# The PEER gate map of a streaming-encoder layer: from one-hot matmuls on TensorE to indirect writes of per-expert totals

## The chip, the cores and the metric

The kernel runs on one core of one Trainium2 chip. The time is that of one execution on the device, in microseconds. A program on one core has one span; the time of an execution is a little longer than that span, since starting and ending it is counted too.

## What is computed

The layer takes 512 frames of 1024 numbers (and 16 meta tokens), runs a token mixer, and then the part that this change touches, a product-key layer of 16384 single-neuron experts ("PEER"). Everything is float32. Cut to what matters:

```python
def peer(x, w_q, sub_keys, u_emb, v_emb):        # x: (512, 1024)
    # two times top 16 of 128 keys for each of 8 heads, then top 16 of their 256 sums
    eidx = ...                                   # (512, 8*16) expert numbers i1*128 + i2
    gate = softmax(sc)                           # (512, 8*16)
    a = einsum('nd,ned->ne', x, u_emb[eidx])     # u: (16384, 1024)
    coef = gelu(a) * gate
    return einsum('ne,ned->nd', coef, v_emb[eidx])
```

One frame can pick the same expert in two heads; then both gates count.

## The kernel before

The kernel doesn't gather for the first 384 frames (`DENSE`, three blocks of 128). It computes all 16384 experts for them: an **up pass** of 128 tiles (a tile is 128 experts), each a product of 24 matmuls of 128x512 (8 slices of the 1024 numbers, three float32r passes each, `three_pass`, L342), a gelu (L1185) and a store to DRAM; then a **down pass** of 128 experts' tiles with 18 matmuls each (L344 to L346 again, from `v_hi`, `v_lo`, `c_hi`, `c_lo`), which adds coefficient times `peer_v` into six PSUM banks. The coefficient is gelu times gate, where the gate is a **gate map** in DRAM: for each (i2, i1) of the 128 x 128 experts a row of 384 frames, nearly all zeros. The last 128 frames go another way: their rows of `peer_v` are gathered by 128 indirect DMAs (L1919) and their activations by 128 more (L1925), all issued by GpSimd during the down pass, and VectorE adds them up (L1703).

Before the up pass stands `route` (L1194), in which queries, key scores and the two top-16 stages run, with the first 24 up tiles between them. Its tail works block by block: VectorE compares (`hits`), GpSimd multiplies (L1517), VectorE sums (`sums`, L1435) into `picked`, the numbers i1 and i2 of every slot. TensorE then transposes i1, i2 and gates of the block (L1317 to L1319) and ScalarE copies them to `i1_t`, `i2_t`, `g_t`. Three up tiles stand between two such blocks.

In `experts` (L1565) VectorE splits the gates into three bfloat16 parts, and in each of the first 24 steps it builds one-hot rows for 16 frames (L1654, L1657, L1660); TensorE turns them into 16 frames of gate map with 48 matmuls of 128x128 in bfloat16 (L1754); ScalarE copies four banks to `gate_stage` (L1798); SyncE stores them (L1858). The last 32 up tiles never go to DRAM: VectorE multiplies them at once by their gates (`keep`, L1669) and keeps them in SBUF as `resident_coef`. The down pass takes those 32 first (`order`), so it can begin with no load but `peer_v`, and its first four tiles are split during the last eight up tiles.

Order on each engine is the order of the code. An engine's instructions wait on semaphores; SyncE issues nearly all loads and stores in one queue, so what stands behind a wait of its waits too. Two raw slots, two hi and two lo slots carry the up tiles; `RING` = 4 slots carry `v_raw`, `v_hi`, `v_lo`, `act_in` and `gate_in` in the down pass.

## Time and profile before

| | us |
|---|---|
| median of 3 runs | 1928.85 |
| lowest and highest | 1923.22, 1933.78 |
| the profiled execution's own time | 1916.39 |
| its span | 1914.5 |
| TensorE matmuls busy | 1815.5 (95%) |
| VectorE busy | 1184.6 (62%) |
| ScalarE busy | 668.0 (35%) |
| GpSimd busy | 579.2 (30%) |

The stages, by the trace: mixer and projections to about 464 us, `route` to 742, one-hot steps to 949, the rest of the up pass to 1379, the down pass to 1902, and a last norm. The granted clock of TensorE was 0.971 of full in the mean. The profile's page gives busy time by engine and by 40 slices of the span; a group is all instructions of one line, operation and tile. Busy time of TensorE is not work at its peak, since matmuls overlap: a matmul of 0.39 us starts every 0.227 us.

### The profile page before, as it was taken

To read this page: it belongs to the slowest core of one execution; us is meant where nothing else is said; L and a number is where in the kernel's file an instruction comes from. 1 tells how busy PE (TensorE), PEld (TensorE's weight loads), DVE (VectorE), ACT (ScalarE), POOL (GpSimd) and SP (SyncE) were. 2 spreads that over 40 slices of the span, in tenths; PEclk is the share of its full clock that TensorE was granted. 3 is DMA by queue.
4 is the path that set the end of the run, shared out by engine and by line. 5 is a ranking of instruction groups with operands and counts; after the bars stand their busy time and mean duration, and the time that the engine had idled before them with its cause. 6 is when DMAs were issued, how large, how long until landed. Compare 5 with 4: busy or idle time off the path is not lost. (4 is left out here: it accounts for less than half of the span.)

```text
span 1914.5 us, 24469 instructions
## 1 busy us (share of the span) xinstructions
PE 1815.5 (95%) x8991; PEld 1491.0 (78%) x8991; DVE 1184.6 (62%) x2275; ACT 668.0 (35%) x1004; POOL 579.2 (30%) x422
## 2 busy tenths in 40 slices
PE   5999999988999689999999999999999999999997
PEld 4877867866788467888888888888888888888885
DVE  3259945542799977888622222232467888888885
ACT  4333203342332223666532222222343333333332
POOL 3644300010544550000000000000177777777820
PEclk9999996988999889999999999999999999999998
DMA  4322110051232333789884444455488999999992
GB/s 136 100 66 56 45 31 1 1 176 55 83 105 78 89 100 109 177 210 235 209 222 148 148 140 146 151 148 188 138 294 269 362 364 372 376 362 372 366 340 88
DMA packets 241690, 337.63 MB, mean 176 GB/s; under 512 B 119856, under 2 KB 178608, under 8 KB 241472
## 3 DMA queue, kind: packets, MB, share of 16 engines
q1 hardware_dynamic: 219088, 269.60, 45.6%
q0 software_dynamic: 22528, 67.19, 9.7%
q8 instruction: 29, 0.48, 0.1%
q14 instruction: 45, 0.37, 0.1%
HBM read 282.19 MB, written 54.53 MB: 176 GB/s over the span
## 5 line engine op out<-in xcount | busy, mean ns | idle before, releaser
L344 PE MATMUL psum<-x_hi,ts_hi_u 128*128 128x512 f32 x1024 | 405.9, 396 | 22.1 <-DVE ts_lo_u L1157 18.9
L346 PE MATMUL psum<-x_hi,ts_lo_u 128*128 128x512 f32 x1024 | 402.4, 393 | 0.0
L345 PE MATMUL psum<-x_lo,ts_hi_u 128*128 128x512 f32 x1024 | 402.2, 393 | 0.0
L1919 POOL DMA_INDIRECT sparse_rows<-in_peer_v,sparse_v_row x128 | 161.5, 1262 | 752.1 <-PE psum L346 662.2
L1157 DVE TENSOR_TENSOR ts_lo_u<-ts_raw_u,ts_hi_u 128x1024 fp32r<-128x1024 f32 x117 | 157.9, 1350 | 370.5 <-ACT ts_hi_u L1152 370.1
L345 PE MATMUL psum<-v_lo,c_hi 128*128 128x512 f32 x768 | 298.8, 389 | 0.0
L346 PE MATMUL psum<-v_hi,c_lo 128*128 128x512 f32 x768 | 298.8, 389 | 0.0
L344 PE MATMUL psum<-v_hi,c_hi 128*128 128x512 f32 x768 | 298.8, 389 | 0.0
L1819 ACT ACTIVATE v_hi<-v_raw 128x1024 fp32r<-128x1024 f32 x128 | 135.8, 1061 | 316.0 <-PE psum L346 276.1
L1185 ACT ACTIVATE ut_out_u<-psum 128x512 f32<-128x512 f32 x128 | 76.6, 598 | 484.1 <-PE psum L346 373.9
L344 PEld LDWEIGHTS psum<-x_hi,ts_hi_u 128*128 128x128 f32 x1024 | 194.6, 190 | 63.5 <-DVE ts_lo_u L1157 19.3
L346 PEld LDWEIGHTS psum<-x_hi,ts_lo_u 128*128 128x128 f32 x1024 | 194.3, 190 | 41.4
L345 PEld LDWEIGHTS psum<-x_lo,ts_hi_u 128*128 128x128 f32 x1024 | 194.5, 190 | 40.0
L1685 DVE TENSOR_TENSOR v_lo<-v_raw,v_hi 128x1024 fp32r<-128x1024 f32 x128 | 157.0, 1226 | 94.3 <-ACT v_hi L1819 71.7
L1925 POOL DMA_INDIRECT sparse_act<-up_acts_sparse,sparse_act_at x128 | 176.1, 1376 | 39.0 <-issue 39.0
L344 PEld LDWEIGHTS psum<-v_hi,c_hi 128*128 128x128 f32 x768 | 144.1, 188 | 30.1
L346 PEld LDWEIGHTS psum<-v_hi,c_lo 128*128 128x128 f32 x768 | 144.1, 188 | 29.9
L345 PEld LDWEIGHTS psum<-v_lo,c_hi 128*128 128x128 f32 x768 | 144.1, 188 | 29.9
L1152 ACT ACTIVATE ts_hi_u<-ts_raw_u 128x1024 fp32r<-128x1024 f32 x128 | 135.1, 1056 | 15.2 <-DMA ts_raw_u<-in_peer_u 15.1
L1157 POOL TENSOR_TENSOR ts_lo_wq<-ts_raw_wq,ts_hi_wq 128x1024 fp32r<-128x1024 f32 x16 | 38.5, 2408 | 291.0 <-ACT ts_hi_wq L1152 290.9
L344 PE MATMUL psum<-whi_in,h_hi 128*128 128x512 f32 (+1 forms) x280 | 110.2, 394 | 2.2 <-PEq L244 2.2
L345 PE MATMUL psum<-wlo_in,h_hi 128*128 128x512 f32 (+1 forms) x280 | 107.9, 385 | 0.0
(231 smaller groups left out, 2636.3 us busy)
## 6 DMA issues: line engine op xcount, KB each, us to landing
ts_raw_u<-in_peer_u SPq DMA_DIRECT2D x128, 512.0 KB, 3.8
v_raw<-in_peer_v SPq DMA_DIRECT2D x128, 512.0 KB
gate_map<-gate_stage SPq DMA_DIRECT2D x48, 512.0 KB, 5.7
up_acts<-ut_out_u SPq DMA_DIRECT2D x96, 192.0 KB, 1.9
act_in<-up_acts SPq DMA_DIRECT2D x96, 192.0 KB
gate_in<-gate_map SPq DMA_DIRECT2D x96, 192.0 KB
raw_in<-in_w_in SPq DMA_DIRECT2D x56, 256.0 KB, 2.8
ts_raw_wq<-in_peer_wq SPq DMA_DIRECT2D x16, 512.0 KB, 4.1
```

Source lines behind the costliest of these rows:

```text
L344: nc.tensor.matmul(out, l_hi, r_hi, start=first, stop=False)
L345: nc.tensor.matmul(out, l_hi, r_lo, start=False, stop=False)
L346: return nc.tensor.matmul(out, l_lo, r_hi, start=False, stop=last)
L1152: nc.scalar.activation(self.hi[:, slot], self.raw[:, slot], ACT.Copy).then_inc(self.hi_done, 1)
L1157: eng_ops.tensor_tensor(self.lo[:, slot], self.raw[:, slot], self.hi[:, slot].bitcast(F32), ALU.subtract).then_inc(self.lo_done, 1)
L1185: nc.scalar.activation(self.out[:, slot], self.bank[slot], ACT.Gelu).then_inc(self.bank_read, 1)
L1685: nc.vector.tensor_tensor(dn.v_lo[:, i], dn.v_raw[:, i], dn.v_hi[:, i].bitcast(F32), ALU.subtract).then_inc(v_lo_done, 1)
L1819: nc.scalar.activation(dn.v_hi[:, i], dn.v_raw[:, i], ACT.Copy).then_inc(v_hi_done, 1)
L1919: nc.gpsimd.indirect_dma_start(dn.rows[:, r], None, v_rows, bass.IndirectOffsetOnAxis(sparse["v_row"][:, j:j + 1], 0)).then_inc(row_in[r], 16)
L1925: nc.gpsimd.indirect_dma_start(dn.picked[:, j:j + 1], None, places, bass.IndirectOffsetOnAxis(sparse["act_at"][:, j:j + 1], 0)).then_inc(p ...
```

## The change

The gate map is made without TensorE. In `route`, GpSimd clears a tile of zeros and SyncE writes it over the whole map in 32 stores of 768 KB, two behind each of the 16 routing steps. `route` keeps `picked` as expert numbers (`expert`) and as addresses in the map (`gate_at`); transposes and their copies go. In `experts`, VectorE makes for every slot of the first 384 frames one `scalar_tensor_tensor` over the 128 slots of its frame: 1 where the other slot has the same expert, times its gate, summed into `total`. So all slots that name one expert hold the same total, and GpSimd writes them with 384 indirect DMAs of 128 x 4 bytes, in whatever order they land. The map is the same as before.

`resident_coef` goes too: all 128 tiles are stored, the down pass goes in the order 0 to 127 and loads gelu and gate for each. `v_raw`, `act_in` and `gate_in` get 8 slots (`RAW`). The first four down tiles are split around the last up tile, and SyncE loads the first coefficients only when all 384 writes have landed.

```diff
@@ route, SyncE
+            sp.wait_ge(zeros_done, 1)
             for j in range(2, G + 2):
                 load_q(j)
...
                 for t in ups[n]:
                     next_up(t)
+                for x in range(n * ZERO_STORES // STEPS, (n + 1) * ZERO_STORES // STEPS):
+                    store_zeros(x)
@@ route, TensorE (and its three copies on ScalarE)
-                pe.wait_ge(picked_done, b + 1)
-                nc.tensor.transpose(bank[:, 0:P], picked[:, b % 2, 0].rearrange(flat), ident[:])
-                nc.tensor.transpose(bank[:, P:2 * P], picked[:, b % 2, 1].rearrange(flat), ident[:])
-                nc.tensor.transpose(bank[:, 2 * P:3 * P], gates[:, b].rearrange(flat), ident[:]).then_inc(turned, 1)
@@ experts, VectorE
+            def total_gate(m, b, j):
+                if m >= 2:
+                    dve.wait_ge(totalled, m - 1)
+                nc.vector.scalar_tensor_tensor(out=dn.same[:, j % 2], in0=expert[:, b], scalar=expert[:, b, j:j + 1],
+                                               in1=gates[:, b].rearrange("p h k -> p (h k)"), op0=ALU.is_equal,
+                                               op1=ALU.mult, accum_out=dn.total[:, b, j:j + 1]).then_inc(totalled, 1)
...
             for n in range(TILES):
-                if n < STEPS:
-                    one_hots(n, n % 2)
                 if n + 2 < TILES:
                     ut.split_lo(nc.vector, dve, n + (R + 2), n % 2)
-                if n >= FIRST_KEPT:
-                    keep(n)
-                if n >= LEAD and (n - LEAD) % 2:
-                    low((n - LEAD) // 2)
+                for m in range(n * TOTALS, min((n + 1) * TOTALS, DENSE_BLOCKS * SLOTS)):
+                    total_gate(m, *place(m))
+            for e in range(EARLY):
+                product(e)
+                low(e)
@@ experts, TensorE
-                    ut.product(nc, pe, x_hi, x_lo, it * 2 + (R + par + 1), 1 - par, False)
-                    rows(it * 2 + par, par, False)
+                    ut.product(nc, pe, x_hi, x_lo, it * 2 + (R + par), par, False)
@@ experts, ScalarE
+            for n in range(TILES):
+                if n == TILES - 1:
+                    for e in range(EARLY):
+                        split_down(e)
                 finish_up(n)
                 next_split(n)
@@ experts, SyncE
-                if n == LEAD - 2:
-                    for e in range(RING):
+                if n == TILES - 2:
+                    for e in range(RAW):
                         load_v(e)
+                    for b in range(DENSE_BLOCKS):
+                        sp.wait_ge(scattered[b], 16 * SLOTS)
+                    for i in range(2):
+                        sp.wait_ge(ut.stored[i], 16 * (RAW // 2))
+                    for e in range(RAW):
+                        load_coef(e)
                 ut.store(sp, acts_d, acts_s, R + n, n % 2)
@@ experts, GpSimd
+            pool.wait_ge(zeroed, 16 * ZERO_STORES)
+            for m in range(DENSE_BLOCKS * SLOTS):
+                b, j = place(m)
+                h, k = divmod(j, PEER_TOPK)
+                if h and k == 0:
+                    pool.wait_ge(scattered[b], 16 * PEER_TOPK * h)
+                pool.wait_ge(totalled, m + 1)
+                scatter_gate(b, j)
             pool.wait_ge(ut.product_done, NKEYS)
```

What this moves is shown at three places, as the instructions stand in a row on one engine. First VectorE at the start of `experts`, before (`val` and `one` are the one-hot tiles, `ts_lo_u` the low half of an up tile):

```order
L1638 TENSOR_TENSOR g_part_b<-g_rest,g_part_f 128x384
L1710 CAST key_twice<-i_t 128x384 x4
L1713 COPY g_twice<-g_part_b 128x384 x6
L1157 TENSOR_TENSOR ts_lo_u<-ts_raw_u,ts_hi_u 128x1024
L1654 TENSOR_TENSOR one<-iota_b,key_twice 128x2048
L1657 TENSOR_TENSOR one<-iota_b,key_twice 128x2048
L1660 TENSOR_TENSOR val<-one,g_twice 128x2048 x3
L1157 TENSOR_TENSOR ts_lo_u<-ts_raw_u,ts_hi_u 128x1024
```

And the same place now:

```order
L1152 TENSOR_TENSOR ts_lo_u<-ts_raw_u,ts_hi_u 128x1024 x2
L1591 SCALAR_TENSOR_TENSOR same_expert,gate_total<-expert,gates 128x128 x10
L1152 TENSOR_TENSOR ts_lo_u<-ts_raw_u,ts_hi_u 128x1024
L1591 SCALAR_TENSOR_TENSOR same_expert,gate_total<-expert,gates 128x128 x10
L1152 TENSOR_TENSOR ts_lo_u<-ts_raw_u,ts_hi_u 128x1024
```

The conversions and the one-hot tiles are gone, and behind each `ts_lo_u` stand ten short sums, until 384 are made. Second, SyncE's queue where up pass and down pass meet, before:

```order
L1869 DMA up_gate<-gate_map 128x384
L1875 DMA v_raw<-in_peer_v 128x1024 x4
L1191 DMA up_acts_sparse<-ut_out_u 128x128
L1145 DMA ts_raw_u<-in_peer_u 128x1024
L1869 DMA up_gate<-gate_map 128x384
```

That piece stands ten tiles ahead of the end of the up pass. The same queue now, two tiles ahead of its end:

```order
L1185 DMA up_acts_sparse<-ut_out_u 128x128
L1725 DMA v_raw<-in_peer_v 128x1024 x8
L1732 DMA act_in<-up_acts 128x384
L1733 DMA gate_in<-gate_map 128x384
L1732 DMA act_in<-up_acts 128x384
L1733 DMA gate_in<-gate_map 128x384
```

The first coefficients (`act_in`, `gate_in`) stand behind eight loads of 512 KB and behind the wait for GpSimd's writes. Third, GpSimd's own order from the end of `route` into `experts`, before (a branch is the passage from one block of the program to the next):

```order
L1517 TENSOR_TENSOR hit<-hit,idx_f 128x2048 x8
L1255 UNCONDITIONAL_BRANCH
L1909 UNCONDITIONAL_BRANCH
L1919 DMA sparse_rows<-in_peer_v,sparse_v_row 128x1024 x4
L1925 DMA sparse_act<-up_acts_sparse,sparse_act_at 128x1 x8
```

and now:

```order
L1509 TENSOR_TENSOR hit<-hit,idx_f 128x2048 x8
L1249 UNCONDITIONAL_BRANCH
L1756 UNCONDITIONAL_BRANCH
L1779 DMA gate_map<-gate_total,gate_at 6291456x1 x384
L1767 DMA sparse_rows<-in_peer_v,v_row 128x1024 x4
```

All 384 writes stand ahead of the first gathered row.

## Rows read from the trace of the kernel before

**Rows 1.** The page, by 40 slices: TensorE busy, in tenths.
```profile
PE   5999999988999689999999999999999999999997
```

**Rows 2.** Windows: busy us (x instructions) of each engine, clock, DMA share, GB/s.
```profile
800.00:850.00 50.00, 50.00 (x436) 42.90 (x435) 43.50 (x39) 33.17 (x38) 0.00 (x0) 1.00 0.94 229
1000.00:1050.00 50.00, 50.00 (x223) 41.39 (x222) 12.04 (x10) 13.92 (x19) 0.00 (x0) 1.00 0.47 146
1600.00:1650.00 50.00, 50.00 (x223) 41.39 (x222) 43.26 (x54) 19.01 (x26) 37.38 (x28) 1.00 1.01 371
```

**Rows 3.** ScalarE by time: gelus that end up tiles (start, us, engine, line).
```profile
764.40 0.60 ACT L1185 ACTIVATE ut_out_u<-psum 128x512 f32<-128x512 f32 x1 [2.83 <-PE psum L346]
772.64 0.60 ACT L1185 ACTIVATE ut_out_u<-psum 128x512 f32<-128x512 f32 x1 [2.81 <-PE psum L346]
...
1324.91 0.60 ACT L1185 ACTIVATE ut_out_u<-psum 128x512 f32<-128x512 f32 x1 [3.89 <-issue]
1330.35 0.60 ACT L1185 ACTIVATE ut_out_u<-psum 128x512 f32<-128x512 f32 x1 [3.89 <-issue]
```

**Rows 4.** Tail of `route`, TensorE: the first of three transposes, a slowed matmul, the next block.
```profile
678.64 0.33 PE L1317 MATMUL psum<-ident,picked 128*128 128x128 f32 x1 [2.43 <-DVE picked L1435]
...
679.69 0.63 PE L346 MATMUL psum<-x_hi,ts_lo_u 128*128 128x512 f32 x1
...
743.40 0.47 PE L344 MATMUL psum<-x_hi,ts_hi_u 128*128 128x512 f32 x1 [2.05 <-PEq L1255]
```

**Rows 5.** The same tail, ScalarE: gelus of its third and its last up tile, and the next.
```profile
676.25 0.60 ACT L1185 ACTIVATE ut_out_u<-psum 128x512 f32<-128x512 f32 x1 [24.70 <-PE psum L346]
...
741.39 0.60 ACT L1185 ACTIVATE ut_out_u<-psum 128x512 f32<-128x512 f32 x1 [3.89 <-PE psum L346]
...
750.72 0.60 ACT L1185 ACTIVATE ut_out_u<-psum 128x512 f32<-128x512 f32 x1 [7.79 <-PE psum L346]
```

**Rows 6.** VectorE: short operations over 128 slots, and the low half of an up tile.
```profile
739.22 0.28 DVE L1445 SCALAR_TENSOR_TENSOR act_row<-picked 128x128 f32<-128x128 f32 x1
739.42 0.28 DVE L1447 TENSOR_TENSOR frame_diag<-ident,iota 128x128 f32<-128x128 f32 x1
...
1326.49 1.23 DVE L1157 TENSOR_TENSOR ts_lo_u<-ts_raw_u,ts_hi_u 128x1024 fp32r<-128x1024 f32 x1 [3.75 <-ACT ts_hi_u L1152]
```

**Rows 7.** GpSimd's indirect DMAs: the whole group, then two single ones.
```profile
L1925 POOL DMA_INDIRECT sparse_act<-up_acts_sparse,sparse_act_at x128 | 176.1, 1376 | 39.0 <-issue 39.0
...
1385.29 0.95 POOL L1925 DMA_INDIRECT sparse_act<-up_acts_sparse,sparse_act_at  x1 [0.30 <-issue]
...
1403.69 1.57 POOL L1925 DMA_INDIRECT sparse_act<-up_acts_sparse,sparse_act_at  x1 [0.31 <-issue]
```

**Rows 8.** SyncE's queue and ScalarE in `route`: one load, and the split that needs it.
```profile
529.46 0.44 SPq L1145 DMA_DIRECT2D ts_raw_wq<-in_peer_wq  x1
...
534.88 1.05 ACT L1152 ACTIVATE ts_hi_wq<-ts_raw_wq 128x1024 fp32r<-128x1024 f32 x1
539.86 0.60 ACT L1185 ACTIVATE ut_out_u<-psum 128x512 f32<-128x512 f32 x1 [3.92 <-PE psum L346]
```

**Rows 9.** SyncE's loads of `v_raw` and the `ts_raw_u` behind, and its reader.
```profile
1328.58 1.86 SPq L1875 DMA_DIRECT2D v_raw<-in_peer_v  x4
...
1331.35 0.81 SPq L1145 DMA_DIRECT2D ts_raw_u<-in_peer_u  x1
...
1338.43 1.06 ACT L1152 ACTIVATE ts_hi_u<-ts_raw_u 128x1024 fp32r<-128x1024 f32 x1 [2.04 <-DMA ts_raw_u<-in_peer_u]
```

**Rows 10.** The page's groups: VectorE's work for a down tile (busy us, mean ns).
```profile
L1685 DVE TENSOR_TENSOR v_lo<-v_raw,v_hi 128x1024 fp32r<-128x1024 f32 x128 | 157.0, 1226 | 94.3 <-ACT v_hi L1819 71.7
...
L1678 DVE TENSOR_TENSOR coef<-act_in,gate_in 128x384 f32<-128x384 f32 x96 | 53.1, 554 | 0.0
```

**Rows 11.** The page's DMA issues: count, size, median us from issue to landing.
```profile
up_acts<-ut_out_u SPq DMA_DIRECT2D x96, 192.0 KB, 1.9
...
ts_raw_wq<-in_peer_wq SPq DMA_DIRECT2D x16, 512.0 KB, 4.1
```

More of the change, by code:

```diff
@@ L1728, in _ @@
             for e in range(EARLY, NKEYS):
-                if e >= RESIDENT:
-                    product(e)
+                product(e)
                 low(e)
@@ L1745, in _ @@
         def _(pe):
-            def rows(n, par, first):
-                pe.wait_ge(hot_done, n + 1)
-                for r in range(STEP):
-                    q, at = divmod(r, BANKROWS)
-                    if at == 0 and not first:
-                        pe.wait_ge(staged, n * banks - (banks - 1 - q))
-                    out = psum[:, q, at * P:(at + 1) * P]
-                    for x in range(PARTS):
-                        last = nc.tensor.matmul(out, gm.one1[:, par, r], gm.val2[:, par, x, r], start=x == 0,
-                                                stop=x == PARTS - 1)
-                    if at == BANKROWS - 1:
-                        last.then_inc(mapped, 1)
             def down(e, i, first, final):
@@ L1793, in _ @@
         def _(act):
-            def copy_rows(n, at, par):
-                for q in range(banks):
-                    act.wait_ge(mapped, n * banks + (q + 1))
-                    nc.scalar.activation(
-                        gm.stage[:, par, :, bass.ds(at + q * BANKROWS, BANKROWS)].rearrange("p i n -> p n i"),
-                        psum[:, q, :].rearrange("p (n i) -> p n i", i=NKEYS), ACT.Copy).then_inc(staged, 1)
             def finish_up(n):
-                if n >= FIRST_KEPT + 2:
-                    act.wait_ge(kept, kept_at(n) - 1)
                 ut.gelu(nc, act, R + n, n % 2)
@@ L1903, in _ @@
             sp.dma_start(g_final[:], io["norm_final"][0:1, :].broadcast_to([P, D])).then_inc(g_final_in, 16)
-            for e in range(RING, NKEYS):
+            for i in range(2):
+                sp.wait_ge(ut.stored[i], 16 * (NKEYS // 2))
+            for e in range(RAW, NKEYS):
                 load_v(e)
-                if e >= RESIDENT:
-                    load_coef(e)
+                load_coef(e)
         @block.gpsimd
```

319 lines of the change are left out of this document (99 added, 220 removed).

## The prediction

> **What bounds the kernel now.** I read the page's slices first: TensorE stands at nine tenths from slice 17 to the end [rows 1], so from there the time is the number of its matmuls, and whatever leaves TensorE leaves the time. Then windows, to see what a stage holds: in the one-hot stage 436 matmuls start in 50 us, in the plain up pass 223, at full clock in both [rows 2]. The gelus at the ends of up tiles give the price: one tile each 8.24 us in the one-hot stage, one each 5.44 us later [rows 3]. Earlier, the tail of `route` is where TensorE has holes: it waits 2.43 us for `picked` before the first transpose, and behind that hole its matmuls take 0.63 us, not 0.39, which is the lower of its two clock levels (1.2 GHz against 2.4) [rows 4]. The down pass is TensorE's too, with VectorE at 43.3 of 50 us and the DMA engines at 371 GB/s and a busy share of 1.01 beside it [rows 2]. So three things could become the bound once TensorE is lighter: VectorE, the memory, and GpSimd, which gets a long new task.
>
> **Part 1, the one-hot stage goes.** 24 steps x (8.24 - 5.44) us = 67.2 us [rows 3], all of it TensorE's, none hidden. ScalarE's copies, VectorE's one-hot tiles and the map's 48 stores lay beside it and are worth nothing by themselves. VectorE's conversions at the start of `experts` lay beside an up tile: nothing. The kept coefficients go, and their 32 multiplications, also beside TensorE: nothing.
>
> **Part 2, the transposes go.** From the gelu at 676.25 to that at 741.39 TensorE does nine up tiles in 65.1 us [rows 5], at 5.44 us each they need 49.0: 16.2 us are lost, in three holes and the slow stretches behind them. Now TensorE doesn't wait for `picked`, but for `ts_lo_u`, which stands on VectorE among `hits` and `sums`. Stepping the chain through (VectorE adds a sum of 4.5 us and hits of 5.5 us per block, with its `ts_lo_u` drawn out while GpSimd multiplies) I get two small holes of about 1.5 and 0.5 us, and perhaps 2 us of slow clock behind each. So 10 of the 16 us come back; bounds 5 and 14. The new address operations cost VectorE 0.6 us a block and are counted in. The 19 us hole before the 676 tile stays, as nothing in front of it changes. The passage into `experts` stays too: a wait of 2.05 us [rows 4] and a first tile of 7.3 us from 743.40 to 750.72 [rows 4, 5].
>
> **Part 3, the zeros.** 32 stores of 768 KB, 25 MB, two behind each routing step, in SyncE's queue ahead of the next query tile. At 371 GB/s [rows 2] two of them take 4.2 us. TensorE is full there, so lateness counts. The tightest load: issued at 529.46, its split starts at 534.88 [rows 8], and such a load takes 4.1 us [rows 11], so it has 1.3 us to spare; the split, and GpSimd's 2.4 us behind it, are done 1.5 us ahead of the gelu at 539.86 that ends the tile in front. With 4.2 us plus 1 us of issuing ahead of it, it comes some 0.8 us too late for TensorE. The pattern stands there three times: 2 us. Below: 0, if the stores land in a lull. Above: 6 us, if each of the three also lets the clock fall (1.9 us as behind the hole at 743, where a tile took 7.3 and not 5.44 us).
>
> **Part 4, the sums on VectorE.** 384 operations over 128 slots, ten per up tile. The nearest row is a `scalar_tensor_tensor` of the same width, 0.28 us, with the next one starting 0.20 us later [rows 6]. Ten take 2 to 3 us, and the split of 1.23 us [rows 6] makes 3.2 to 4.2 of 5.44 us. Nobody waits: nothing, as long as one takes under 0.42 us.
>
> **Part 5, the 384 writes on GpSimd.** This is the part that decides. They begin with the first sums, behind the split that follows the first tile of `experts`: about 10 us after TensorE starts there (7.3 for the tile, 1.05 and 1.2 for the splits, 0.5 more). From TensorE's start to the end of the up pass are 7.3 + 103 x 5.44 = 567.6 us. SyncE comes to the wait for the writes about 5.7 us before that end (two tiles less the gelu and two stores, then eight loads of 0.47 us each [rows 9]). Less 2 us for the last write to land, 550 us are left, 1.43 us each. The price: an indirect DMA that nothing holds up takes 0.95 us and 0.30 us pass to the next: 1.25 us [rows 7]. One that meets a running VectorE operation takes 1.57 us [rows 7]; the mean of all in the down pass is 1.376 + 0.30 = 1.68 us [rows 7], with VectorE at 87% [rows 2]. In the up pass VectorE is at 24% (12.0 of 50 us [rows 2]) for two thirds of the time and at some 70% with operations of a quarter of that length before. About one in four then waits 0.6 us: 1.37 to 1.42 us each. That makes 534 us, and 16 us to spare. I take nothing for it; both ends, 1.25 us (nothing) and 1.68 us (95 us late), are far apart, and I take the near end because these two differ by how long VectorE holds on, and it holds on little here.
>
> What the small pieces cost: a step of the one-hot stage puts 4096 pieces of 256 bytes in DRAM and raises the DMA engines' work from 0.47 x 5.44 to 0.94 x 8.24 us x 16 [rows 2, 3], so a small piece costs 83 / 4096 = 0.02 us. Eight pieces of 4 bytes per engine and write may take 0.18 us each before they hold GpSimd up. The Trainium skill (DMA: Bandwidth & Descriptors, "Specifications") says that below 512 bytes the DMA engine reads, modifies and writes; it gives no price for it, and the map's 256-byte pieces paid it already, if it is paid.
>
> **Part 6, the handover.** Before, the down pass began 0.5 us behind the last up tile, with no coefficient to load. Now coefficient 0 stands behind eight loads of `v_raw`. The rate: five loads of 512 KB and 0.26 MB beside them, 2.9 MB, were in 9.85 us after the first issue [rows 9], with 1.9 us for the way [rows 11]: 365 GB/s. Eight loads, two stores and the first pair are 4.84 MB: 15.2 us from an issue at 9.4 us before the up pass's end, so 5.8 us after it. Then the product 0.55, `v_lo` 1.23 [rows 10] and `c_lo`, as wide as the product, 0.55 us: 8.1 us. GpSimd's gathered rows share the memory from the end of the up pass on: 2 us. The clock falls in the hole: 1.9 us. Together 12 us; bounds 8 (no sharing, no clock) and 18 (sharing by halves). Behind it tiles are ready at one per 2.5 us against 4.08 that TensorE takes.
>
> **Part 7, the down pass.** 32 more pairs are loaded. Per tile 896 KB and 1.12 gathered rows of 512 KB are 1.51 MB in 4.08 us, 369 GB/s, for 114 tiles, not for some 85. TensorE's 223 matmuls per 50 us beside 371 GB/s [rows 2] say that this is kept up, and eight slots, not four, give more slack. Nothing. VectorE's sum per tile is what it was for 96 tiles.
>
> The sum: -67.2 - 10 + 2 + 12 = -63 us. On the profiled execution's own 1916.39 us (1.9 over its span) that is 1853; the median of the runs lies 12.5 us above that execution, so I add there: 1928.85 - 63 = 1866 us.
>
> **Rivals.** *GpSimd is the bound, slower.* The writes cost what the indirect DMAs of the down pass cost, 1.68 us. For: it is the mean of 128 rows, and short VectorE operations may hold it up as often as long ones. Against: VectorE's share. The down pass starts 10 + 645 + 2 us, then 5.6 us for a pair and its splits and 1.9 us of clock, after TensorE's start, against 567.6: 97 in place of 12 us, so +22: 1951 us. It costs from 1.43 us on and is slower than before from 1.62 us on. *The same, half way:* 1.50 us each is 28 in place of 12 us: 1882 us. *The small writes land slowly* and GpSimd's waits on `scattered` bite: no row shows one of 4 bytes; by the 0.02 us it can't be, at over 0.18 us each it gives times like the first rival's. *VectorE is the bound of the up pass:* with an operation at 0.50 us, for the sum that it also writes out, 39 tiles take 0.8 us longer: 1897 us. *The memory is the bound of the down pass.* If 369 GB/s can't be held over 114 tiles, the lead is eaten up and TensorE waits. Against: 85 tiles at 371 GB/s without a wait. The Trainium skill (DMA: Bandwidth & Descriptors, "Where 436 GB/s comes from") has about 358 GB/s as the memory's limit for a core: by that the 172 MB of those 114 tiles take 480 us, not 465, and the time would be up to 15 us more, 1881. The trace's 371 GB/s is above that limit, and I go by the trace. *It doesn't do what it says:* TensorE's tiles stay at 5.44 us only if the splits aren't held up by sums; that is the VectorE case.
>
> **Chances.** Forecast 0.60; half way 0.15; GpSimd bound 0.11; slow small writes 0.05; VectorE 0.06; memory 0.03. Parts at their best ends give 1856, at their worst 1881. The range takes in half way, VectorE and memory, and 5 us for the spread of the runs: 1848 to 1902. A difference under 0.5% can't be told from none here; faster 0.84, same 0.05, slower 0.11.
>
> **What would show it.** Right: gelus each 5.44 us from the first tile of `experts` on; no one-hot matmul; GpSimd's writes 1.35 to 1.42 us apart, the last some 15 us before SyncE's first `act_in`; a hole of about 10 us at the first down matmul, and `route`'s tail 10 us shorter. Wrong: gaps over 1.43 us, with ScalarE or SyncE waiting for GpSimd ahead of the down pass; gelus more than 5.44 us apart; holes between query tiles while zeros are stored.

## The result: 15% slower, not 3% faster

The changed kernel takes 2215.6 us (median of 4 runs, 2205.3 to 2223.9) against 1926.1 us beside it: a ratio of 1.149, 95% interval 1.143 to 1.155. The forecast was 1866 us. It was wrong in sign and by 350 us.

The slices of TensorE on the page of the changed kernel, to be read against [rows 1]:

```profile
PE   5999999889986838516476139999997999999997
```

TensorE is down from slice 15 to slice 24 (a slice is 55.3 us, so from 775 to 1328 us), the first 560 us or so of `experts`, and back at nine tenths behind them. The windows of the changed kernel (columns as in [rows 2]) say what runs in that stretch:

```profile
761.00:1000.00 239.00, 124.62 (x418) 92.14 (x417) 69.31 (x371) 26.61 (x35) 170.48 (x165) 0.71 0.21 58
1000.00:1310.00 310.00, 152.75 (x507) 110.81 (x506) 81.78 (x429) 32.26 (x42) 223.63 (x217) 0.70 0.19 53
1320.00:1660.00 340.00, 340.00 (x1501) 281.62 (x1500) 76.06 (x62) 97.05 (x125) 0.00 (x0) 1.00 0.49 150
```

While GpSimd (fifth count: 165 and 217 of its 384 writes) writes the gate map, TensorE does half its work, and no engine is full: VectorE 27%, ScalarE 11%, the DMA engines 20% at 53 to 58 GB/s. Behind the last write the up pass runs as forecast, 1501 matmuls in 340 us, 5.44 us a tile.

The 299 us of difference between the spans (2213.8 and 1914.5), cut at the last gelu of `route` and the first `c_lo` matmul of the down pass: `route` ends 8.0 us later (749.36 against 741.39, [rows 5]); the up pass of `experts` takes 285.9 us more (to 1673.4 against 1379.6); the down pass 5.3 us more.

Where TensorE's time goes, by the groups of the changed kernel (busy us, mean ns, then the idle time before and what ended it):

```profile
L339 PE MATMUL psum<-x_hi,ts_hi_u 128*128 128x512 f32 x1024 | 426.4, 416 | 219.3 <-DVE ts_lo_u L1152 110.6 <-issue 82.9 <-ACT ut_out_u L1180 19.2
...
L341 PE MATMUL psum<-x_hi,ts_lo_u 128*128 128x512 f32 x1024 | 420.7, 411 | 45.5 <-issue 45.4
L340 PE MATMUL psum<-x_lo,ts_hi_u 128*128 128x512 f32 x1024 | 420.6, 411 | 42.7 <-issue 42.7
...
L1779 POOL DMA_INDIRECT gate_map<-gate_total,gate_at x384 | 397.1, 1034 | 187.5 <-issue 110.5 <-DVE same_expert L1591 76.7 <-remote 0.3
...
L1591 DVE SCALAR_TENSOR_TENSOR same_expert<-expert,gates 128x128 f32<-128x128 f32 x384 | 108.2, 348 | 2.8 <-DVE same_expert L1591 2.4 <-issue 0.3
...
L1180 ACT ACTIVATE ut_out_u<-psum 128x512 f32<-128x512 f32 x128 | 76.5, 598 | 854.2 <-PE psum L341 462.9 <-DMA mixed<-in_x 371.8 <-issue 19.5
```

Of the idle time before the gelus, 371.8 us end with a DMA's landing (part of that time they would have waited for TensorE anyway). The name that the profile gives it, `mixed<-in_x`, is that of another transfer; the only DMAs for which line 1180 waits are the stores of the tile two before. One such wait, from SyncE's, TensorE's and ScalarE's timelines:

```profile
768.81 0.32 SPq L1184 DMA_DIRECT2D up_acts<-ut_out_u  x1
```
```profile
796.05 0.58 PE L341 MATMUL psum<-x_hi,ts_lo_u 128*128 128x512 f32 x1 [1.47 <-issue]
```
```profile
808.00 0.60 ACT L1180 ACTIVATE ut_out_u<-psum 128x512 f32<-128x512 f32 x1 [27.30 <-DMA mixed<-in_x]
```

The tile was ready at 797, the store two tiles back had been issued at 769, and the gelu comes at 808. Before, such a store landed 1.9 us after its issue [rows 11]; here it is seen after 39 us.

The transfer itself was not late. In the trace of the DMA engines' packets the last data of the two stores is through by 770.7, and the last of their 32 completion packets (4 bytes each, 16 for each store) goes out then too. While the gelu and all behind it wait, from 784 to 808 us, SyncE's queue has no packet at all, and GpSimd's is the only one with any:

```profile
DMA packets 620, 0.01 MB, mean 0 GB/s; under 512 B 620, under 2 KB 620, under 8 KB 620
q0 software_dynamic: 620, 0.01, 1.9%
```

So the delay lies between the completion packet and the engine that waits for it, not in the data's way. TensorE also stands still in the middle of a tile, where the program has no wait (column: start, duration; in brackets the idle time before):

```profile
817.78 0.39 PE L340 MATMUL psum<-x_lo,ts_hi_u 128*128 128x512 f32 x1 [2.27 <-issue]
820.59 0.59 PE L341 MATMUL psum<-x_hi,ts_lo_u 128*128 128x512 f32 x1 [2.42 <-issue]
```

These stops are a good part of the loss: the idle time before L340 and L341, which have no wait, comes to 88 us.

GpSimd itself runs as forecast, 1.03 us a write and 0.30 us to the next, as long as it has sums to write. With the tiles late the sums come late too, so over the whole the 384 writes start 1.44 us apart in the mean.

### The profile page after: what moved, and what is told of

Read it like the earlier page. It is cut to its first block and busy times, and to the rows that moved or that the text cites. A ratio compares the mean times of both kernels' runs of the same rounds, so it can differ in the third digit from the quotient of the medians.

```text
span 2213.8 us, 23017 instructions
## 1 busy us (share of the span) xinstructions
PE 1826.3 (82%) x7830; PEld 1464.9 (66%) x7830; DVE 1162.5 (53%) x2914; ACT 576.2 (26%) x899; POOL 981.5 (44%) x807
## 5 line engine op out<-in xcount | busy, mean ns | idle before, releaser
L339 PE MATMUL psum<-x_hi,ts_hi_u 128*128 128x512 f32 x1024 | 426.4, 416 | 219.3 <-DVE ts_lo_u L1152 110.6
L1152 DVE TENSOR_TENSOR ts_lo_u<-ts_raw_u,ts_hi_u 128x1024 fp32r<-128x1024 f32 x117 | 170.7, 1461 | 684.3 <-ACT ts_hi_u L1147 610.8
L1779 POOL DMA_INDIRECT gate_map<-gate_total,gate_at x384 | 397.1, 1034 | 187.5 <-issue 110.5
L341 PE MATMUL psum<-x_hi,ts_lo_u 128*128 128x512 f32 x1024 | 420.7, 411 | 45.5 <-issue 45.4
L340 PE MATMUL psum<-x_lo,ts_hi_u 128*128 128x512 f32 x1024 | 420.6, 411 | 42.7 <-issue 42.7
L339 PEld LDWEIGHTS psum<-x_hi,ts_hi_u 128*128 128x128 f32 x1024 | 205.5, 201 | 284.0 <-issue 179.9
L1767 POOL DMA_INDIRECT sparse_rows<-in_peer_v,v_row x128 | 168.1, 1313 | 436.0 <-PE psum L341 347.4
L341 PE MATMUL psum<-v_hi,c_lo 128*128 128x512 f32 x768 | 300.0, 391 | 0.8 <-issue 0.8
L340 PE MATMUL psum<-v_lo,c_hi 128*128 128x512 f32 x768 | 299.7, 390 | 1.0 <-issue 1.0
L341 PEld LDWEIGHTS psum<-x_hi,ts_lo_u 128*128 128x128 f32 x1024 | 205.4, 201 | 95.4 <-issue 51.6
L340 PEld LDWEIGHTS psum<-x_lo,ts_hi_u 128*128 128x128 f32 x1024 | 205.6, 201 | 91.5 <-issue 49.9
L1773 POOL DMA_INDIRECT sparse_act<-up_acts_sparse,act_at x128 | 173.8, 1358 | 55.0 <-issue 38.7
L341 PEld LDWEIGHTS psum<-v_hi,c_lo 128*128 128x128 f32 x768 | 144.7, 188 | 31.5 <-issue 1.4
L340 PEld LDWEIGHTS psum<-v_lo,c_hi 128*128 128x128 f32 x768 | 144.9, 189 | 31.2 <-issue 1.2
```

Source lines behind the costliest of these rows:

```text
L339: nc.tensor.matmul(out, l_hi, r_hi, start=first, stop=False)
L340: nc.tensor.matmul(out, l_hi, r_lo, start=False, stop=False)
L341: return nc.tensor.matmul(out, l_lo, r_hi, start=False, stop=last)
L1152: eng_ops.tensor_tensor(self.lo[:, slot], self.raw[:, slot], self.hi[:, slot].bitcast(F32), ALU.subtract).then_inc(self.lo_done, 1)
L1767: nc.gpsimd.indirect_dma_start(dn.rows[:, r], None, v_rows, bass.IndirectOffsetOnAxis(places["v_row"][:, j:j + 1], 0)).then_inc(row_in[r], 16)
L1773: nc.gpsimd.indirect_dma_start(dn.picked[:, j:j + 1], None, act_cells, bass.IndirectOffsetOnAxis(places["act_at"][:, j:j + 1], 0)).then_in ...
```

## Experiments: is it the writes, and what about them?

Each kernel is the changed one with the edit shown, unless said otherwise. The kernel of before took 1912.8 to 1925.8 us beside them. A time without a count is that of a single execution; 13 executions of the kernel of before on chip 13 lay between 1914.7 and 1933.2 us. First the writes left out:

```diff
-            for m in range(DENSE_BLOCKS * SLOTS):
-                ...
-                scatter_gate(b, j)
-                    for b in range(DENSE_BLOCKS):
-                        sp.wait_ge(scattered[b], 16 * SLOTS)
```

> The 384 indirect writes of the gate map, and the waits on their arrival, are left out (the map stays at its zeros, so the coefficients are wrong); VectorE still sums the totals, the zero stores, the new route tail, the stores of all up tiles and the new down pass stay. In the trace of the changed kernel the up pass of the experts begins at 751 us and ends at 1667; 104 tiles at 5.44-5.47 us would take 569 us. Theory W (the writes alone hold the up pass up): up pass 751 to about 1320, time about 1869 us, and the waits of ScalarE's gelus for stored tiles vanish. Rival S (the sums on VectorE or the longer stores slow the up pass, whatever the writes do): over 2000 us.

Measured: 1862.8 us. The up pass is clean, and the gelus wait for nothing but TensorE. The first line is the window, the second the gelus' group:

```profile
800.00:1000.00 200.00, 200.00 (x884) 165.62 (x883) 127.58 (x645) 56.74 (x74) 0.00 (x0) 1.00 0.48 145
```
```profile
L1180 ACT ACTIVATE ut_out_u<-psum 128x512 f32<-128x512 f32 x128 | 76.6, 598 | 522.0 <-PE psum L341 522.0
```

So the loss hangs on GpSimd's 384 transfers: the sums, the zeros, the longer stores and the new down pass are all still there. Next, reads in their place:

```diff
-                    gate_cells, bass.IndirectOffsetOnAxis(places["gate_at"][:, b, j:j + 1], 0),
-                    dn.total[:, b, j:j + 1], None).then_inc(scattered[b], 16)
+                    dn.read[:, b, j:j + 1], None, gate_cells,
+                    bass.IndirectOffsetOnAxis(places["gate_at"][:, b, j:j + 1], 0)).then_inc(scattered[b], 16)
```

> Each of the 384 indirect writes becomes an indirect read of the same 128 cells of 4 bytes, into a scratch tile of SBUF, with the same waits and the same order on GpSimd (the map stays at its zeros). Theory W (what hurts is writing 49152 cells of 4 bytes to DRAM): about 1870 us, like the kernel without writes. Rival Q (what hurts is GpSimd issuing indirect transfers back to back for 500 us, whatever way the bytes go): about 2200 us.

Measured: 2193.8 us. My own theory, that small writes to DRAM hurt, fell here. Then the place of the pieces, and their number:

```diff
-                    nc.vector.tensor_scalar(places["gate_at"][:, b], number, float(DENSE),
+                    nc.vector.tensor_scalar(places["gate_at"][:, b], iota[:], float(DENSE),
```

> The same 384 indirect writes of 128 pieces of 4 bytes, but write (b, j) goes to row j of the map: its 128 pieces lie side by side in 512 bytes (the map is wrong). Theory W-count (the number of small pieces is what costs): about 2215 us. Theory W-spread (it is that every piece goes to another place of DRAM): near 1870 us, with the gelus 5.44 us apart while GpSimd writes.

Measured: 2239.5 us; where the pieces go makes no difference.

```diff
-                    gate_cells, bass.IndirectOffsetOnAxis(places["gate_at"][:, b, j:j + 1], 0),
-                    dn.total[:, b, j:j + 1], None)
+                    gate_cells, bass.IndirectOffsetOnAxis(places["gate_at"][0:32, b, j:j + 1], 0),
+                    dn.total[0:32, b, j:j + 1], None)
```

> The same 384 writes back to back, but each covers only partitions 0 to 31: 32 pieces of 4 bytes instead of 128 (three quarters of the map stay at their zeros). The number of transfers and of completion increments stays. The runs so far: 1863 us without the writes, 2194 with reads in their place, 1861 with 200 writes 2.7 us apart. Theory P (the burden is the 128 pieces of each transfer, for which GpSimd has to write descriptors): under 1900 us. Theory D (the burden is each transfer as such, its start and its 16 increments): 2150 us or more, since GpSimd would issue at the same pace or faster.

Measured: 2225.8 us. A quarter of the pieces costs as much as all. So between 32 and 128 pieces it is the number of transfers (or of their 16 completions) that counts, not that of pieces or bytes. The same issue without the list of places:

```diff
-                nc.gpsimd.indirect_dma_start(
-                    gate_cells, bass.IndirectOffsetOnAxis(...), dn.total[:, b, j:j + 1], None)
+                nc.gpsimd.dma_start(
+                    gates_d.rearrange("e p f -> (e p) f")[j, b * P:(b + 1) * P].unsqueeze(1),
+                    dn.total[:, b, j:j + 1])
```

> Each of the 384 indirect writes becomes a plain write that GpSimd issues: write (b, j) puts the same 128 cells of 4 bytes side by side into row j of the map (the map is wrong). Theory Q (any transfers that GpSimd issues at this pace hold the rest up): about 2200 us, if GpSimd's time per issue is again near 1.3 us. Rival I (only the indirect form does it): about 1865 us.

Measured: 2066.4 us, between the two. It is another loss: no gelu waits for a store, but ScalarE waits 320.7 us for `ts_raw_u`, and the DMA engines are full at a fifth of their rate. Its window, then its wait:

```profile
800.00:1000.00 200.00, 127.86 (x456) 98.97 (x455) 75.12 (x399) 29.57 (x38) 100.77 (x190) 0.80 0.93 76
```
```profile
L1147 ACT ACTIVATE ts_hi_u<-ts_raw_u 128x1024 fp32r<-128x1024 f32 x128 | 134.8, 1054 | 320.7 <-DMA ts_raw_u<-in_peer_u 320.7
```

GpSimd issues 190 in 200 us here, faster than ever in the indirect form, and no gelu is held up by a store. So the late completions of the stores belong to the indirect form; why the plain one fills the DMA engines (0.93 at 76 GB/s) I did not follow up.

Is anything else of the change needed? The kernel of before, with 384 reads added and nothing else:

```diff
+            for m in range(384):
+                if m % 16 == 0 and m >= 48:
+                    pool.wait_ge(extra[m // 16 % 3], 256 * (m // 48))
+                nc.gpsimd.indirect_dma_start(sparse["extra"][:, ...], None, peer_v_cells,
+                    bass.IndirectOffsetOnAxis(sparse["act_at"][:, ...], 0)).then_inc(extra[m // 16 % 3], 16)
             pool.wait_ge(ut.product_done, NKEYS)
```

> The kernel of before, unchanged but for 384 indirect reads of 128 cells of 4 bytes each (cells of peer_v, into a scratch tile that nobody reads), which GpSimd issues back to back from the start of the experts, with the order waits of the changed kernel (each sixteen wait for the sixteen issued 48 earlier). The one-hot stage, the kept coefficients and all else stay. If the burst of indirect transfers alone explains the changed kernel's loss of about 350 us: 1926 + 250 to 350 = 2180 to 2280 us. Rival (it needs the changed kernel's extra stores or its sums on VectorE as well): under 2000 us.

Measured: 2268.9 us. The windows of this kernel hold the next question:

```profile
800.00:1000.00 200.00, 183.66 (x1440) 153.93 (x1438) 128.44 (x112) 108.93 (x120) 163.66 (x120) 0.97 0.83 204
1000.00:1300.00 300.00, 57.81 (x111) 32.30 (x111) 6.13 (x5) 7.71 (x10) 226.83 (x231) 0.52 0.08 17
```

In the one-hot stage VectorE's work stretches GpSimd's reads to 1.67 us each (120 in 200 us) and TensorE keeps 92%. Behind it they come every 1.30 us (231 in 300 us), and TensorE keeps 19%.

## Experiments: at what pace?

200 of the 384 writes, two behind each up tile (the rest of the edit is the count):

```diff
...
+                if m % 2 == 0:
+                    pool.wait_ge(ut.product_done, R + m // 2)
                 scatter_gate(b, j)
```

> Only 200 of the 384 writes are made (the rest of the map stays at its zeros), two for each up tile, released by TensorE's finished tile, so that a write comes every 2.7 us rather than every 1.3 us. In the changed kernel the up pass lost about 347 us to 384 writes, 0.90 us each. If each write costs its share whatever the rate: 1869 + 200 x 0.90 = about 2050 us. If a queue builds up only because the writes come faster than DRAM takes them in: under 1900 us, with no gelu waiting for a store.

Measured: 1861.5 us. Nothing lost, with 200 writes made. So the loss isn't a price per write. With `m % 3` and `m // 3`, and 300 writes:

> 300 of the 384 writes, three for each up tile, released by TensorE's finished tile: bursts of three, one write every 1.8 us on average (84 writes are left out, their cells stay zero). Two a tile cost nothing (1861 us). If there is a limit of rate between 1.3 and 1.8 us a write, under 1880 us; if a burst of three is already too much, or the limit lies above 1.8 us, over 1950 us.

Measured: 1875.6 us; TensorE has 500 of 500 us from 800 on. Then VectorE's sums spread evenly, here over all 384 writes and 102 tiles:

```diff
-                for m in range(n * TOTALS, min((n + 1) * TOTALS, DENSE_BLOCKS * SLOTS)):
+                for m in range(*(min(x, TILES - 2) * DENSE_BLOCKS * SLOTS // (TILES - 2) for x in (n, n + 1))):
```

> The changed kernel whole, with all 384 writes, but VectorE sums three or four totals behind each of 102 up tiles instead of ten behind each of the first 39, so that GpSimd gets a write every 1.45 us on average rather than issuing back to back at 1.27 to 1.33 us. If what GpSimd issues is worked off at a pace between 1.3 and 1.45 us a transfer and only the backlog hurts: 1865 to 1890 us, a kernel faster than both. If the limit lies above 1.45 us: the up pass stays slow over its whole length, and the time is 2100 us or more.

Measured: 1930.7 us (10 runs; ratio 1.003, 1.000 to 1.006). Between my two cases: with the sums handed out evenly, so that a write comes every 1.45 us as long as a tile takes 5.44 us, the changed kernel got back 285 of the 353 us that part it from the one without writes. The same with 340 writes over 100 tiles:

> Like the even version with 384 writes (1931 us), but 340 writes behind 100 up tiles: one every 1.60 us on average (44 writes are left out, their cells stay zero). Even pacing at 1.45 us was too fast, 1.81 us was clean (1876 us). If the limit lies near 1.5 us: under 1880 us, and GpSimd never waits for writes that it issued long before. If it lies near 1.7 us: over 1900 us.

Measured: 1870.9 us. The windows of these two, side by side (the even one first). By then the writes of both come 1.6 us apart (186 and 188 in 300 us): in the even one the up pass has slowed down, and the sums, and so the writes, with it.

```profile
1000.00:1300.00 300.00, 277.27 (x1182) 224.72 (x1181) 111.29 (x417) 76.58 (x98) 192.22 (x186) 0.98 0.44 129
```
```profile
1000.00:1300.00 300.00, 300.00 (x1326) 248.39 (x1325) 120.51 (x430) 85.55 (x111) 200.66 (x188) 1.00 0.49 145
```

| writes as the program hands them out, at 5.44 us a tile | mean distance in the trace | writes | time, us | before beside it, us | chip |
|---|---|---|---|---|---|
| two a tile | 2.67 us | 200 | 1861.5 | 1920.9 | 2 |
| three a tile, together | 1.80 us | 300 | 1875.6 | 1925.8 | 13 |
| evenly, every 1.60 us | 1.60 us | 340 | 1870.9 | 1918.3 | 6 |
| evenly, every 1.45 us | 1.62 us | 384 | 1930.7 | 1925.8 | 13 |
| back to back, 1.3 us | 1.44 us | 384 | 2215.6 | 1926.1 | not on record |
| back to back, 1.3 us, reads | 1.46 us | 384 | 2193.8 | 1920.9 | 2 |

Where the up pass suffers, the distance in the trace is longer than that handed out, since late tiles hold up the sums. So the second column is partly an effect; what sets the rows apart is the first.

A queue worked off at some 1.5 us a transfer would give such a table (an estimate from its first column). Bursts of 48, then a pause, should tell:

```diff
-            for m in range(DENSE_BLOCKS * SLOTS):
+            for m in range(300):
+                if m % 48 == 0:
+                    pool.wait_ge(ut.product_done, R + m // 3)
```

> 300 of the 384 writes, like the run with three a tile (1876 us, one per 1.8 us on average), but in bursts of 48 back to back behind every sixteenth up tile (84 writes are left out). Theory C (a backlog that is worked off at about 1.5 us a transfer): a burst of 48 at 1.27 us leaves about 7 transfers or 11 us behind, gone before the next burst: 1875 to 1920 us. Rival B (while GpSimd issues back to back everything slows at once, whatever came before): 300 of 384 writes' share of 350 us, so about 2140 us.

Measured: 2109.9 us, near the rival's 2140. Three windows, in the first burst, behind it, and in the second:

```profile
780.00:820.00 40.00, 13.83 (x34) 8.67 (x33) 6.17 (x37) 1.54 (x2) 28.90 (x31) 0.63 0.11 29
840.00:880.00 40.00, 40.00 (x178) 33.14 (x177) 28.12 (x150) 12.34 (x16) 0.96 (x1) 1.00 0.46 143
900.00:940.00 40.00, 10.87 (x24) 6.35 (x24) 3.95 (x21) 1.54 (x2) 30.55 (x32) 0.62 0.09 20
```

The burst begins at 757 and TensorE holds out for some 10 to 20 writes (11.0 of 11 us to 768, 7.4 of 12 us from there to 780); from 780 it falls to a third, and 10 to 20 us behind the burst all is well. 247 us are lost to 300 writes, 0.82 us each, as in the changed kernel (353 to 384, 0.92 each). A mere backlog of 48 x (1.5 - 1.27) = 11 us can't do that. So the theory of a simple queue falls too: what fits is that it counts how fast GpSimd issues for some 10 to 20 transfers in a row (threes are harmless, 48 are not; nothing between was run).

And alone? On the kernel without writes, behind the down pass, 96 reads back to back beside a chain of loads:

```diff
+            for m in range(24):
+                if m:
+                    sp.wait_ge(alone_v, 16 * m)
+                sp.dma_start(dn.v_raw[:, 0], io["peer_v"][:, m]).then_inc(alone_v, 16)
...
+            pool.wait_ge(alone_v, 16 * 4)
+            for m in range(96):
+                nc.gpsimd.indirect_dma_start(
...
```

> The kernel without the 384 writes (1863 us), with a stretch added behind the down pass, in which nothing else runs: SyncE loads one 512 KB tile of peer_v after the other, 24 in all, each issued when the one before has landed; from the fourth on GpSimd issues 96 indirect reads of 128 cells back to back (about 1.26 us each, 121 us), and six tiny memsets show when each sixteen have landed. Theory C (completions of all transfers pile up behind what GpSimd issues too fast, whatever else runs): the reads land at 1.4 to 1.6 us each, the last some 20 to 30 us after its issue, and SyncE's loads, 3 to 5 us apart before, come 10 to 30 us apart during the burst. Rival M (it takes the up pass's own stores, loads and semaphores beside it): the reads land within 3 us of their issue, and the loads stay 3 to 6 us apart.

The whole took 2009.9 us, with the added stretch in it. Its queue of SyncE, and GpSimd's last read and the memsets that wait for the landings:

```profile
1851.47 81.82 SPq L1761 DMA_DIRECT2D v_raw<-in_peer_v  x24
```
```profile
1985.36 0.95 POOL L1810 DMA_INDIRECT alone_read<-up_acts_sparse,act_at  x1 [0.30 <-issue]
1986.31 0.23 POOL L1815 MEMSET alone_mark<- 128x1 f32 x5
1987.87 0.10 POOL L1815 MEMSET alone_mark<- 128x1 f32 x1 [1.33 <-DMA alone_read<-up_acts_sparse,act_at]
```

When the last read is issued the first 80 have landed, and it lands itself within 1.6 us of the end of its issue. The loads come 3.4 us apart (81.8 / 24), with 20 of them beside the reads. So the same pace, 1.25 us, does no harm beside one load at a time and idle engines, on a chip (6) on which reads beside the up pass cost 350 us: it takes something of the up pass beside it. What that is isn't shown.

## Experiments: a merged store, and another chip

The guess behind these was that all transfers together have a limit: 6.4 per 5.44 us had been clean, 6.8 not. One store per up tile instead of two would bring the changed kernel below it:

```diff
-        sp.dma_start(acts_d[n], self.out[:, slot, 0:DENSE]).then_inc(self.stored[slot], 16)
-        sp.dma_start(acts_s[n], self.out[:, slot, DENSE:FRAMES]).then_inc(self.sparse_stored[slot], 16)
+        sp.dma_start(acts_d[n], self.out[:, slot]).then_inc(self.stored[slot], 16)
...
```

> The changed kernel whole, with ten totals a tile and GpSimd writing back to back as before, but each up tile is stored by one transfer of 256 KB instead of two (192 and 64 KB): the map of activations has 512 columns, the dense loads read 384 of them, the gathers of the sparse block the last 128. The bytes are the same. Theory N (what is limited is the number of transfers on the core, whoever issues them; clean so far up to 6.4 per 5.44 us, 1.18 per us, and not clean at 6.8): the burst would have 4.1 indirect writes and 2 others per tile, 6.1, so it is clean: 1860 to 1880 us. Rival G (only the pace of GpSimd's indirect transfers counts): 2200 us as in the changed kernel.

Measured: 1862.6 us (4 runs), ratio 0.972, interval 0.970 to 0.974. With the even sums, 1.45 us apart:

> As the run before, with VectorE's totals spread over 102 tiles, so that GpSimd writes every 1.45 us on average. With two stores a tile this took 1931 us. Theory N: 3.76 writes and 2 others per tile, 5.8 transfers, below the limit: 1860 to 1875 us. Rival G: 1931 us again.

Measured: 1866.0 us, ratio 0.975 (0.973 to 0.976). The third run of that group was meant to confirm it from the other side, with two more stores of 8 KB behind each tile of the kernel that writes three a tile:

```diff
                 ut.store(sp, acts_d, acts_s, R + n, n % 2)
+                for x in range(2):
+                    sp.dma_start(more_d[2 * n + x], ident[:, 0:16]).then_inc(more_stored, 16)
```

> The run with three writes a tile (300 of 384 writes, 1876 us, 6 transfers per tile), with two more stores of 8 KB per up tile that SyncE issues and nobody reads: 8 transfers per tile, GpSimd's pace unchanged. Theory N: the limit of 6.4 to 6.8 transfers per tile is passed, so the up pass stretches by a fifth at least (113 us): 1990 us or more. Rival G (only GpSimd's pace counts): under 1900 us.

Measured: 1868.3 us. 8 transfers a tile, and nothing lost: on this chip a count of all transfers is refuted, though its two forecasts before had come true (by luck, on the reading that follows). So three runs took the merged store apart again. Both stores, the first still of 256 KB:

> The faster version (1863 us: one 256 KB store per up tile, GpSimd writing back to back) with the second store of 64 KB put back beside it, into a tensor that nobody reads, waited for by the gelu two tiles later as in the changed kernel. Against the changed kernel only the first store differs (2048 bytes per partition instead of 1536). If the second store is what the burst collides with: 2150 to 2250 us. If it was the 1536-byte pieces of the first: 1860 to 1880 us.

Measured: 1865.0 us. The changed kernel whole, with two more stores of 8 KB a tile, as in the diff above:

> The changed kernel whole (two stores per tile, ten totals a tile, GpSimd back to back: 2216 us) with two more 8 KB stores per up tile from SyncE that nobody reads. With GpSimd at 1.8 us a write these two more stores cost nothing (1868 us). If more transfers beside the burst make it worse: over 2230 us. If extra stores leave it as it is: 2190 to 2240 us. Under 2000 us would say that no count of transfers explains it.

Measured: 1867.1 us. The merged store with one more of 64 KB that no engine waits for:

> The faster version (1863 us) with one more store of 64 KB per up tile, from the unchanging identity tile into a tensor that nobody reads, for which no engine waits until the up pass is over: the same three transfers per tile from SyncE as in the changed kernel, but no second wait on ScalarE. If it is the third transfer as such: about 2200 us. If it is the gelu's second wait that turns late completions into lost time: under 1900 us, while the run with both stores waited for is slow.

Measured: 1860.9 us. All clean, the changed kernel with two added stores too, in which GpSimd issues no more slowly (384 writes 1.37 us apart in the mean, with no wait for late sums). Its window and its gelus, to be held against the changed kernel's at the top:

```profile
800.00:1000.00 200.00, 200.00 (x884) 165.62 (x883) 128.45 (x645) 60.09 (x74) 155.57 (x146) 1.00 0.53 149
```
```profile
L1180 ACT ACTIVATE ut_out_u<-psum 128x512 f32<-128x512 f32 x128 | 76.5, 598 | 487.7 <-PE psum L341 487.7
```

No count of transfers, and nothing about the second store, explains this, unless added stores cure what they were expected to worsen. There is another difference. These six kernels were run on one chip, number 9, and later than all others; all slow ones ran on other chips (2, 13 and 6; the number of the first measurement's chip isn't on record, it may be one of these). The pages tell the chips apart in code that is the same in all of them. In the down pass, the median time from issue to landing is left out where the trace lacks too many completions. The even run with 340 writes (chip 6), then the run just shown (chip 9):

```profile
ts_raw_u<-in_peer_u SPq DMA_DIRECT2D x128, 512.0 KB
v_raw<-in_peer_v SPq DMA_DIRECT2D x128, 512.0 KB
```
```profile
ts_raw_u<-in_peer_u SPq DMA_DIRECT2D x128, 512.0 KB, 3.8
v_raw<-in_peer_v SPq DMA_DIRECT2D x128, 512.0 KB, 6.4
```

Counted in the traces over the down pass's last 350 us (completions recorded against completion packets sent): 0.74 to 0.81 in all fourteen kernels of the earlier runs, without exception, and 1.00 in all six of chip 9. Three writes a tile left 0.68 of the completions of 800 to 1200 us recorded on chip 13, and 0.97 on chip 9 with two stores more. So my reading is that chip 9 takes the same burst without harm, and the merged store has no part in it. That is argued from the traces, not shown by a run: the changed kernel itself was not run on chip 9, nor the merged store on one of the others. Whether the merged store helps on them stays open, and so does what differs between the chips. And if chip 9 is immune, its six kernels say nothing on what counts on the others: there a limit on all transfers together is as open as one on GpSimd's pace.

A rival that no run touches is the recording itself: every execution on record has the profiler's span and clock, and none was made without them, so nothing tells whether the stops are there unrecorded. Against it, though weakly: with a fifth of the completions missing the down pass on the same chips runs at full pace.

## Why the prediction was wrong, point by point

**The step that failed** is part 5, where the 384 writes were costed by their duration on GpSimd and by what small pieces cost the DMA engines, and by nothing else. Neither was off: 1.37 us from one write to the next in the clean kernel with all 384 (1.37 to 1.42 forecast), 1.33 in the changed one where no sum is waited for, and a DMA share of 0.2. What was missing is a third cost, put at nothing without a row for it and borne by others: on every chip used but number 9 an indirect transfer every 1.3 us beside the up pass makes completions seen late (39 us instead of 1.9) and stalls TensorE in mid-tile. It costs the up pass nothing at 1.60 us (579.4 us against 577.4 without writes) and 0.92 us per write at 1.3. That the writes cause it is shown by leaving them out; why completions are seen late stays open. The margin of "16 us to spare" was computed for a GpSimd that may issue as fast as it can.

**The rival that came nearest,** small writes that land slowly (5%), had the symptom, late completions, and the wrong cause: reads and a quarter of the pieces do the same. Its price, 1951 us, counted only GpSimd's own waits. What the Trainium skill says of writes below 512 bytes (DMA: Bandwidth & Descriptors, "Specifications") plays no part that shows: reads cost the same.

**Parts 1 and 6** (-67.2 and +12) are right where the writes do no harm. From `route`'s last gelu to the first `c_lo` matmul, 638.2 us before, the kernel without writes takes 577.4 and the changed one with two more stores 581.8: -61 and -56 against a forecast of -55. The hole at the handover was forecast with 8 to 18 us. In the changed kernel, then in the one with two more stores:

```profile
1672.40 0.79 PE L339 MATMUL psum<-v_hi,c_hi 128*128 128x512 f32 x1 [11.32 <-DVE c_lo L1610]
```
```profile
1327.84 0.80 PE L339 MATMUL psum<-v_hi,c_hi 128*128 128x512 f32 x1 [12.54 <-DVE c_lo L1612]
```

**Part 2** (-10) was mis-sized. From the third tile's gelu to the last, [rows 5], the tail takes 61.0 us instead of 65.1: 4 us came back. Two gaps stayed that I had put at 1.5 and 0.5 us, with 2 us of slow clock each; they cost 5.2 and 6.9 us. The second, from the gelu at 720.70:

```profile
733.04 0.60 ACT L1180 ACTIVATE ut_out_u<-psum 128x512 f32<-128x512 f32 x1 [10.79 <-PE psum L341]
```

TensorE waits there for `ts_lo_u`, which VectorE makes while GpSimd multiplies.

**Part 3** (+2, at most 6) was too small. The tail begins 12.1 us later (688.32 against 676.25). 3.1 us of that stand already at the first gelu (504.92 against 501.83; over the kernels it comes between 495 and 504 us); the other 9 lie between the first gelu and the tail, as they do in every kernel with the change (6.8 to 10.1 us). The query loads beside the zeros take 6.5 us to land, not 4.1 [rows 11]:

```profile
gate_map<-zeros SPq DMA_DIRECT2D x32, 768.0 KB, 5.8
```
```profile
ts_raw_wq<-in_peer_wq SPq DMA_DIRECT2D x16, 512.0 KB, 6.5
```

I had looked for lateness in three places, not in all. And the sum there doesn't come out of its own terms: 4.2 + 1 us ahead of a load with 1.3 and 1.5 us to spare make it 2.4 us late, not 0.8, and three times that is 7 us. No run left the zeros out, so that they are the cause is argued. Parts 2 and 3 together: +8.0 us at the end of `route` (+4.8 without writes, +5.6 with two more stores) against a forecast of -8.

**Part 4** (nothing) is right: 0.348 us and 0.083 us for a second instruction that reads the accumulator, which I had not counted, partly overlapped; ten sums take 2.7 us. **Part 7** (nothing) is right: from the first `c_lo` matmul to the last the down pass takes 521.6 us before, and 523.9 and 523.0 us in these two kernels. On the chips other than 9 the kernels with writes take 526 to 531 us, those paced without loss too (527 to 530). The changed kernel's 5.3 us more are spent right behind the handover, where GpSimd gathers back to back (from 1670 to 1720 us TensorE has 45.5 of 50 us, and 100 of 100 behind it):

```profile
1670.00:1720.00 50.00, 45.48 (x184) 36.51 (x185) 29.86 (x42) 18.57 (x26) 24.80 (x23) 0.91 0.95 333
1720.00:1820.00 100.00, 100.00 (x443) 82.79 (x442) 88.84 (x109) 37.79 (x51) 76.66 (x57) 1.00 1.02 378
```

Without the burst's side effect the sum was off by 11 to 17 us: -63 forecast, -52.4 for the merged store (1862.6 against 1915.0 on its chip) and -45.7 for the changed kernel with two more stores (1867.1 against 1912.8). Most of it, 13 to 14 us, is from parts 2 and 3.

## What to carry to other kernels

GpSimd's indirect transfers have a price that doesn't stand in their own row: cost them by how many come in a row and how fast, beside what, and pace them (here, let the engine that feeds them feed them evenly) rather than let them run. Pacing has a price too: 384 writes at the harmless 1.60 us need 614 us, more than the 568 of the up pass, and off chip 9 no kernel with all 384 was faster than before (the even one: ratio 1.003). A stretch in which every engine and the DMA engines idle while everybody waits for transfers issued long ago is the sign of it. Where a change is measured on one chip and its fix on another, nothing is known of the fix: run the slow kernel again beside it.

## What the runs showed of the hardware

- Indirect transfers of GpSimd at 1.3 us each beside a busy up pass cut TensorE's busy time to between a fifth and a half on chips 2, 6 and 13 and in the first measurement, whether they read (2193.8 us) or write (2215.6 us), and with 32 pieces (2225.8 us) as with 128. At 1.60 us the up pass loses nothing. Beside single loads and idle engines even 1.25 us costs nothing, and the last lands within 1.6 us.
- A store whose last completion packet went out at 770.7 us let its waiter go at 808 us, with SyncE's queue empty in between.
- Chip 9 took the same pace without loss (1867 us with two more stores a tile; 1863 and 1865 us in other forms), and its traces hold all completions where those of the others lack a fifth.
- The kernel of before had the sign in its trace: its page has a landing time for `ts_raw_u`, 3.8 us, and none for `v_raw`, whose loads run beside GpSimd's gathers.
- Plain writes of 128 pieces of 4 bytes, one per 1.05 us, fill the DMA engines (share 0.93 at 76 GB/s); the indirect form of the same writes leaves them at 0.47 with the same places, and at 0.21 in the changed kernel.
